# A transformer kernel in three-pass fp32: feed-forward input projections by seven half-size products, on one core

## What is computed

```python
def swiglu(h, w_in, w_out):                  # w_in 1024 x 5632, w_out 2816 x 1024
    gate, up = split(h @ w_in, 2)
    return (silu(gate) * up) @ w_out

# first block, latent tokens x (512 x 1024)
x = x + mod2 * rms_norm(gla_mixer(modulate(rms_norm(x), mod0, mod1)))
h = modulate(rms_norm(x), mod3, mod4)
x = x + mod5 * rms_norm(swiglu(h, ffn_w_in, ffn_w_out))         # ffn0
# second block
x = x + 0.5 * swiglu(rmsnorm(x) * g1, [ffn1_w1 ffn1_w3], ffn1_w2)   # ffn1
x = x + mixer(rmsnorm(x) * gm) @ w_out
x = x + 0.5 * swiglu(rmsnorm(x) * g2, [ffn2_w1 ffn2_w3], ffn2_w2)   # ffn2
return rmsnorm(x) * gf
```

## Time and profile before

| | before |
|---|---|
| three runs, median (us) | 1607.99, 1608.75, 1610.84; 1608.75 |
| span of the profiled execution (us) | 1607.1 |
| lies between the span and the median of the runs (us) | 1.65 |
| TensorE busy | 1596.4 us, 99% |
| VectorE, ScalarE, GpSimd busy | 849.0, 502.5, 119.9 us |
| the chain that ended last | TensorE 99% |
| DMA | 171.35 MB, 107 GB/s on average |

### The profile page before, as it was taken

One profiled execution on the slowest core, in us unless ns is written; L12 is line 12 of the kernel. 1 busy time (PEld: TensorE's weight loads), 2 busy tenths in 40 slices (PEclk: granted clock), 3 DMA queues, 4 the chain that ended last, 5 costly groups with the idle time before them and its releaser, 6 DMA issues.

```text
span 1607.1 us, 19314 instructions
## 1 busy us (share of the span) xinstructions
PE 1596.4 (99%) x7785; PEld 1343.6 (84%) x7785; DVE 849.0 (53%) x1050; ACT 502.5 (31%) x589; POOL 119.9 (7%) x106
## 2 busy tenths in 40 slices
...
GB/s 388 193 156 159 208 53 53 80 79 96 87 104 104 66 89 98 116 79 105 99 84 104 91 73 105 98 146 103 80 53 79 105 104 94 89 104 69 95 100 77
DMA packets 30647, 171.35 MB, mean 107 GB/s; under 512 B 3200, under 2 KB 5504, under 8 KB 17152
## 3 DMA queue, kind: packets, MB, share of 16 engines
...
HBM read 168.47 MB, written 2.10 MB: 106 GB/s over the span
## 4 chain that ended last, share of the span: by engine, by line
PE 99%; issue 0%; DVE 0%; POOL 0%; ACT 0%; POOLq 0%; DVEq 0%
PE bank L515 98%; PE bank L814 0%; PE bank L870 0%; POOL root L420 0%; PE bank L738 0%; PE bank L1143 0%; DVE y_ffn L2534 0%; ACT tmp L1500 0%; POOLq L123 0%; DVE qd L2111 0%; DVE kd L2111 0%; DVE tmp L2091 0%; DVE y_ffn L2532 0%; ACT mod_rows L1289 0%; DVEq L123 0%
## 5 line engine op out<-in xcount | busy, mean ns | idle before, releaser
L515 PE MATMUL bank<-a_hi,w_all 128*128 128x512 f32 x2490 | 764.7, 390 | 0.0
L515 PEld LDWEIGHTS bank<-a_hi,w_all 128*128 128x128 f32 x2490 | 466.5, 188 | 98.8 <-issue 2.5
L1712 DVE TENSOR_TENSOR w_all<-w_raw,w_all 128x2048 fp32r<-128x2048 f32 x140 | 323.3, 2309 | 360.5 <-ACT w_all L1265 360.3
L515 PE MATMUL bank<-a_lo,w_all 128*128 128x512 f32 x1245 | 477.1, 389 | 0.0
L1265 ACT ACTIVATE w_all<-w_raw 128x2048 fp32r<-128x2048 f32 x142 | 271.7, 1913 | 562.7 <-PE bank L515 562.7
L515 PE MATMUL bank<-g_hi,w_all 128*128 128x512 f32 (+1 forms) x1088 | 331.9, 386 | 0.0
L515 PEld LDWEIGHTS bank<-a_lo,w_all 128*128 128x128 f32 x1245 | 233.7, 188 | 48.8 <-issue 0.5
L515 PEld LDWEIGHTS bank<-g_hi,w_all 128*128 128x128 f32 x1088 | 203.9, 189 | 41.2
L515 PE MATMUL bank<-g_lo,w_all 128*128 128x512 f32 (+1 forms) x544 | 210.2, 386 | 0.0
L515 PEld LDWEIGHTS bank<-g_lo,w_all 128*128 128x128 f32 x544 | 102.5, 188 | 20.6
L515 PE MATMUL bank<-w_all,a_hi 128*128 128x512 f32 (+1 forms) x384 | 108.9, 359 | 0.0
...
## 6 DMA issues: line engine op xcount, KB each, us to landing
w_raw<-in_ffn_in SPq DMA_DIRECT2D x66, 1024.0 KB, 4.8
...
mod_raw<-in_mod POOLq DMA_DIRECT2D x16, 1024.0 KB, 5.6
...
w_raw<-in_gla_in SPq DMA_DIRECT2D x10, 1024.0 KB, 5.1
w_raw<-in_mix_in SPq DMA_DIRECT2D x10, 1024.0 KB, 4.7
mod_w<-in_mod SPq DMA_DIRECT2D x8, 1024.0 KB, 18.4
w_raw<-in_gla_out SPq DMA_DIRECT2D x4, 1024.0 KB, 4.7
```

The source lines that it names most:

```text
L515: return pe.matmul(out, lhs, rhs, start=first, stop=last, skip_group_check=True)
L1712: V.tensor_tensor(flat(w_lo[s]), flat(w_raw[s]), flat(w_hi[s]).bitcast(F32), ALU.subtract).then_inc(lo_done[s], 1)
```

## The change

Two of the eleven pairs of each feed-forward stay as they are. Pairs 2 to 10 are computed by Strassen's scheme in Winograd's form, over halves of k, halves of a unit's columns (c0, c1) and halves of the tokens, gate and up unit together: seven products, each of 4 k x 2 units x 3 passes = 24 matmuls of 128x256, 168 a pair. They use banks 0 to 3 (`PRODUCTS`).

- **Weights.** Seven forms of 128x1024: three are parts of the raw tiles, four are sums. GpSimd makes the first two sums (`form_sums`, one in place), VectorE the last two (`form_sum`). Each form is copied by ScalarE (`form_upper`) and subtracted by VectorE (`form_lower`) into a ring of four slots. SyncE loads the next pair's two raw tiles once `form_lower` 4 and 5 of this pair are done.
- **Activations.** Once in each feed-forward the scaled input `hs` (x by gain and roots, on VectorE in ffn1 and ffn2) gets four sums (`sum_x`) and is split into seven forms (`x_hi`, `x_lo`), while TensorE works on the plain pairs.
- **Results.** ScalarE copies four products out of PSUM (`snap`), VectorE makes the four quarters (`combine`), silu and the product work on 128x1024.
- **Output projection.** It runs in three parts of k: (0, 8) after pairs 2 to 4, (8, 16) after pairs 5 to 8, (16, 22) after pairs 9 and 10. Each part's sums are added by VectorE into `y_acc` or `xT`: 24 evictions a feed-forward, not 8. In ffn0 the norm's terms of all eight chunks come in the last part.
- `AHEAD` is gone; dummy matmuls (`keep_busy`) stand there. The loops over pairs are unrolled. In ffn0 ScalarE writes the modulated input twice, into `a_hi` and into `hs`.

The heads of the change:

```diff
-OUT_PARTS = ((0, 6), (6, 12), (12, 17), (17, 22))
...
+PLAIN = 2
+STRETCHES = ((2, 3, 4), (5, 6, 7, 8), (9, 10))
...
+OUT_PARTS = ((0, 8), (8, 16), (16, 22))
...
+PRODUCTS = ((0, True), (1, True), (0, False), (2, True), (0, False), (3, True), (2, False))
...
-AHEAD = (3, 4, 5)
```

SyncE's loads of the raw tiles inside a stretch, and GpSimd's two sums:

```diff
+if r:
+    sp.wait_ge(form_lo, FORMS * (n - 1) + 5 + h)
+else:
+    sp.wait_ge(hi_done[h], cnt.next(hi_done[h]))
+    sp.wait_ge(lo_done[h], cnt.next(lo_done[h]))
+w = slice(h * UNIT // 2, (h + 1) * UNIT // 2)
+sp.dma_start(raw_pair[h][:].rearrange("p u k o -> p u (k o)"),
+             w_in[2 * i:2 * i + 2, :, w].rearrange("u p w -> p u w")).then_inc(raw_loaded[h], 16)
...
+def form_sums(f):
+    for q, groups in enumerate(STRETCHES):
+        for i in groups:
+            n = PAIRS_PER_FFN * f + i - PLAIN
+            raw = 16 * (RAW_BEFORE[f] + PLAIN + i - PLAIN + 1 + 2 * q)
+            pool.wait_ge(raw_loaded[0], raw)
+            pool.wait_ge(raw_loaded[1], raw)
+            if i > PLAIN:
+                pool.wait_ge(form_lo, FORMS * n - 3)
+            nc.gpsimd.tensor_tensor(form_source(3), form_source(4), form_source(5), ALU.add).then_inc(form_summed, 1)
+            pool.wait_ge(form_summed, 4 * n + 1)
+            nc.gpsimd.tensor_tensor(form_source(4), form_source(0), form_source(4), ALU.add).then_inc(form_summed, 1)
```

TensorE's pair, and the dummies in place of the products ahead:

```diff
+def pair(q, r, i):
+    n = PAIRS_PER_FFN * f + i - PLAIN
+    first = i == PLAIN
+    for j, (b, fresh) in enumerate(PRODUCTS):
+        if first:
+            pe.wait_ge(xf_lo, FORMS * f + j + 1)
+        if j == 0:
+            if first:
+                gate_banks_free(i)
+            else:
+                pe.wait_ge(snapped, 4 * n)
+        elif j == 1 and not first:
+            pe.wait_ge(combined, 4 * n - 3)
+        elif j == 2:
+            pe.wait_ge(snapped, 4 * n + 1)
+        elif j == 3:
+            if first:
+                up_banks_free(i)
+            else:
+                pe.wait_ge(combined, 4 * n)
+        elif j == 4:
+            pe.wait_ge(snapped, 4 * n + 2)
+        elif j == 5 and not first:
+            pe.wait_ge(combined, 4 * n - 1)
+        elif j == 6:
+            pe.wait_ge(snapped, 4 * n + 3)
+        pe.wait_ge(form_lo, FORMS * n + j + 1)
+        slot = ring[(STRETCH_SLOT[q] + FORMS * r + j) % 4]
+        for k in range(KD // 2):
+            for u in range(2):
+                m = mm3(bank[b][:, HALVES[u]], (slot[:, 0, u, k], slot[:, 1, u, k]),
+                        (x_form[:, j, k, 0], x_form[:, j, k, 1]), fresh and k == 0 and u == 0, k == KD // 2 - 1)
+        m.then_inc(form_used, 1)
...
-    ahead_products(0, 0, AHEAD[0:2], True, False)
...
+keep_busy((4, 0)[n], (6, 12)[n])
```

ScalarE's pair:

```diff
+def pair(q, r, i):
+    n, last = PAIRS_PER_FFN * f + i - PLAIN, i == STRETCHES[q][-1]
+    form_upper(q, r, i, 3)
+    snap(n, snap_a, 0, 1, 4 * n - 3)
+    if r:
+        pair_silu(i - 1)
+    form_upper(q, r, i, 4)
+    form_upper(q, r, i, 5)
+    if r or q == 0:
+        product_hi(i - 1)
+    snap(n, snap_b, 0, 3, 4 * n)
+    form_upper(q, r, i, 6)
+    snap(n, snap_w, 2, 4, 4 * n - 2)
+    if not last:
+        form_upper(q, r + 1, i + 1, 0)
+    snap(n, snap_c, 0, 5, 4 * n - 1)
+    if not last:
+        form_upper(q, r + 1, i + 1, 1)
+        form_upper(q, r + 1, i + 1, 2)
```

VectorE: the input's sums, the weights' sums and low parts, the first quarters, the pair, the opening of a feed-forward, and the last part of its output (`p` counts pairs of chunks):

```diff
+def scale_x():
+    for m in range(KD):
+        V.scalar_tensor_tensor(hs[:, m], xT[:, m], gains(m), roots[:], ALU.mult, ALU.mult).then_inc(hs_done, 1)
+def sum_x():
+    dve.wait_ge(hs_done, X_STEPS * f + KD)
+    V.tensor_tensor(x_sum[:, 4, :, 1], x_quarter(1, 1), x_quarter(0, 1), ALU.subtract).then_inc(hs_done, 1)
...
+def form_sum(q, i, at):
+    n = PAIRS_PER_FFN * f + i - PLAIN
+    if at == 2:
+        dve.wait_ge(form_summed, 4 * n + 2)
+        dve.wait_ge(form_lo, FORMS * n + 1)
+        out, x, y = form_source(2), form_source(4), form_source(5)
+    else:
+        dve.wait_ge(form_summed, 4 * n + 3)
+        out, x, y = form_source(6), form_source(2), form_source(1)
+    V.tensor_tensor(out, x, y, ALU.add).then_inc(form_summed, 1)
+def form_lower(q, r, i, j):
+    n, slot = PAIRS_PER_FFN * f + i - PLAIN, ring[(STRETCH_SLOT[q] + FORMS * r + j) % 4]
+    dve.wait_ge(form_hi, FORMS * n + j + 1)
+    V.tensor_tensor(slot[:, 1], form_source(j), slot[:, 0].bitcast(F32), ALU.subtract).then_inc(form_lo, 1)
...
+def combine(n, quarter_at):
+    if quarter_at == 0:
+        dve.wait_ge(snapped, 4 * n + 1)
+        dve.wait_ge(form_used, FORMS * n + 2)
+        V.tensor_tensor(quarter(0, 0), by_unit(bank[1]), by_unit(snap_a), ALU.add).then_inc(combined, 1)
+    elif quarter_at == 1:
+        dve.wait_ge(snapped, 4 * n + 4)
+        V.scalar_tensor_tensor(quarter(1, 1), by_unit(snap_c), -1.0, by_unit(snap_w), ALU.mult, ALU.subtract).then_inc(combined, 1)
+    elif quarter_at == 2:
+        dve.wait_ge(form_used, FORMS * n + 6)
+        V.tensor_tensor(quarter(1, 0), by_unit(bank[3]), by_unit(snap_c), ALU.subtract).then_inc(combined, 1)
...
+def pair(q, r, i):
+    n, last = PAIRS_PER_FFN * f + i - PLAIN, i == STRETCHES[q][-1]
+    opening = i == PLAIN
+    if r:
+        combine(n - 1, 3)
+    elif opening:
+        ups(i - 1)
+        form_lower(q, r, i, 2)
+    form_lower(q, r, i, 3)
+    form_lower(q, r, i, 4)
+    if r or opening and scaled:
+        product(i - 1)
+    form_lower(q, r, i, 5)
+    if r or opening:
+        product_lo(i - 1)
+        dve.wait_ge(gated, GROUPS * f + i)
+    combine(n, 0)
+    form_lower(q, r, i, 6)
+    if not last:
+        form_lower(q, r + 1, i + 1, 0)
+        form_lower(q, r + 1, i + 1, 1)
+    else:
+        out_lower(q, 0)
+    combine(n, 1)
+    combine(n, 2)
+    if not last:
+        form_sum(q, i + 1, 2)
+        form_sum(q, i + 1, 3)
+        form_lower(q, r + 1, i + 1, 2)
...
+if f == 0:
+    sum_x()
+    split_lo(0)
+elif f == 1:
+    dve.wait_ge(roots_copied, cnt.next(roots_copied))
+    scale_x()
+    sum_x()
+    gates(0)
+    split_lo(0)
+else:
+    split_lo(1)
+    x_roots(5)
+    gates(0)
+    scale_x()
+ups(0)
+if f:
+    product(0)
+split_lo(1)
+if f == 2:
+    sum_x()
+x_lo(0)
+x_lo(1)
+product_lo(0)
 for j in range(2):
     V.memset(sq_sum[:, j * (T // 2):(j + 1) * (T // 2)], 0.0).then_inc(pair_out[j], 1)
     cnt.expect(pair_out[j])
...
+for j in range(2, FORMS):
+    x_lo(j)
+if scaled:
+    gates(1)
+first_forms(0, PLAIN)
...
+if f:
+    sum_pair((4 + 2 * j, 5 + 2 * j), CPU * p, True, j, f == 2)
+else:
+    for c in range(CPU):
+        m = CPU * p + c
+        dve.wait_ge(out_ready, cnt.next(out_ready))
+        V.tensor_tensor(y_acc[:, m], y_acc[:, m], bank[4 + 2 * j + c][:], ALU.add).then_inc(y_whole, 1)
+if p < 2:
+    out_lower(2, p + 2)
+elif p == 2 and f < 2:
+    split_lo(0)
+if f == 0:
+    for c in range(CPU):
+        m = CPU * p + c
+        done = pair_out[j] if c else chunk_done
+        cnt.expect(done)
+        y_terms_of(1, m, (done, cnt.now(done)), 2 * KD + m + 1)
```

More of the change, by code:

```diff
@@ L216, in build @@
         ret_sq_t = [place(f"ret_sq_t{s}", [P, T], F32, big + (64 + 2 * s) * KB) for s in range(2)]
-        tmp = [place(f"tmp{s}", [P, T]) for s in range(4)]
+        both = place("both", [P, 2, CPU, T])
+        tmp = [both[:, j // CPU, j % CPU] for j in range(4)]
         col4 = place("col4", [P, 16])
@@ L248, in build @@
         bank = [ctx.enter_context(nc.psum_tensor(f"bank{b}", [P, T], F32)) for b in range(8)]
-        ready = [sem(f"bank_ready{b}") for b in range(8)]
+        ready = [sem(f"bank_ready{b}") for b in range(6)]
         free = [sem(f"bank_free{b}") for b in range(8)]
@@ L1084, in half_roots @@
                 m.then_inc(roots_ready, 1)
[L1086 removed]
+            ffn(0)
             term_sums(1)
[L1088 to L1090 removed]
+            keep_busy(0, 20)
+            ffn(1)
             for n in range(6):
@@ L1541, in half_gains, with ffn, silu @@
                     nc.scalar.activation(y_ffn[:, m, h], xT[:, m, h], ACT.Copy, scale=col("final_g", m)).then_inc(y_gained, 1)
[L1543 to L1559 removed]
+            def ffn(f, next_gains=None):
+                scaled = f > 0
+                def silu(i):
@@ L2210, in x_roots, with sum_pair @@
                 dve.wait_ge(roots_copied, cnt.next(roots_copied))
-            def sum_pair(banks, chunks, half, to_x, j, squares):
-                dst = xT if to_x else y_ffn
-                at = [dst[:, chunks[c]] for c in range(CPU)]
-                if len(at[0].shape) == 3:
-                    at = [x.rearrange("p o t -> p (o t)") for x in at]
+            def sum_pair(banks, m0, half, j, squares):
                 for c in range(CPU):
```

673 lines of the change are left out of this document (376 added, 297 removed).

## The result

The changed kernel takes 1632.96 us (median of 4 runs, 1629.96 to 1639.28) against 1609.49 us before: ratio 1.0141, 95% interval 1.0118 to 1.0164. It is slower by 1.4%, and just above the range that was forecast. The profiled executions differ by 26.4 us (spans of 1633.5 and 1607.1); the medians differ by 23.5. What follows explains the 26.4.

What follows compares the result with a forecast made beforehand. TensorE, busy 1596.4 of 1607.1 us, was taken to bound the kernel. Saved 43.2 less lost 39.5 gave net -3.7, a span of 1603.4; with the median 1.65 above it, 1605 us, range 1583 to 1630.

Steps and rivals of the forecast that it cites:

- 27 pairs at 0.120 us a matmul: TensorE's changed pairs: 168 matmuls of 0.120 us, 20.16 us in place of 21.76, saving 43.2 us in all.
- loops inside stretches: Runs of changed pairs: the other engines' loop outlasts TensorE's pair; 11 us lost, bounds 0 and 56.
- ffn1's opening: TensorE waits for VectorE's split behind `scale_x` and `sum_x`, then for the first form; 7.0 us lost, bounds 4 and 10.
- ffn2's opening: VectorE reaches the first form at 1289, TensorE is ready at 1281; 8.3 us lost, bounds 3.5 and 11.
- ffn0's end: All norm terms fall into the last output part, so VectorE ends later after TensorE; 7.9 us lost, bounds 4 and 11.
- `AHEAD` gone: At ffn1's start, 18 matmuls (4.1 us) go back into the first pair; 1.3 us lost, bounds 0 and 4.1.
- last parts of ffn1, ffn2: Third weight part is split behind two evictions, 0.5 and 2.5 us after TensorE wants it; 3 us lost.
- lower clock: New waits of 6 to 8 us can bring TensorE's lower clock level twice more; 1 us lost, bounds 0 and 6.
- load 4.8 ... 21.45 us against TensorE's 20.16: The loop from one `form_lower` 5 to the next: raw tile load 4.8, then sums, forms, quarters; 21.45 us in all.
- no lock: Rival: GpSimd and VectorE don't exclude each other for these strided reads; loop 19.1 us, 1588 us in all; chance 0.20.
- the loop is longer and sets the pace: Rival: GpSimd sums of 2.6 us each make the loop 22.0, 1625 us in all (1650 with 3.3); chance 0.26.
- No saving at all: Rival: a new weight load every 0.12 us holds 128x256 matmuls back to 0.1295 us; 1648 us; chance 0.03.

Runs made afterwards that it cites:

- small_loads: The changed kernel, but from a stretch's second pair on each raw tile load brings only 64 of its 1024 elements a partition and unit; one run, 1602.8 us.
- sums_on_vector: The changed kernel, but from a stretch's second pair on VectorE forms all four weight sums; 1607.03 us against 1610.92 before, ratio 0.9974.

## Why the prediction was wrong, by its own steps

| step | said (us) | measured (us) |
|---|---|---|
| 27 pairs at 0.120 us a matmul | -43.2 | -43.2 |
| loops inside stretches | 11 | 32.0 |
| ffn1's opening | 7.0 | 9.2 (6.6 idle, 2.6 at the lower clock) |
| ffn2's opening | 8.3 | 9.3 (7.6 idle, 1.7 at the lower clock) |
| ffn0's end | 7.9 | 9.7 (join 7.6 longer, output projection 2.2) |
| `AHEAD` gone | 1.3 | 2.1 (ffn1's first pair 22.8, not 20.7) |
| last parts of ffn1, ffn2 | 3 | 5.8 (1.5 and 4.3) |
| lower clock | 1 | in the rows above: 2.6, 1.7, 1.7 in ffn2's last part, some 7 in the loops |
| ffn0's start (not named) | 0 | 1.3 |
| sum | -3.7 | 26.2 of 26.4 |

The mechanism was right, and the loop was mis-sized: it accounts for 21 of the 30 us between forecast and profile (some of it through the lower clock, below). The step that failed is "load 4.8 ... 21.45 us against TensorE's 20.16". Its chain from the landing on was priced at 16.65 us and took 16.7 (409.97 to 426.68). The load was priced by the earlier trace rows, a median over loads that mostly ran alone. Here the second tile is issued 2.3 us behind the first and lands after 5.1 to 6.5 us in ffn0 and ffn2, 6.9 to 8.1 in ffn1. Such a term enters every turn: past 20.16 each us of the loop is paid in each of the nine steady turns, and with ffn1's 24 us the lead of a stretch's second pair is gone too. The prediction said itself that the loop decides above 21.9; it took 22.5 in ffn0 and some 24 in ffn1. small_loads and sums_on_vector, each taking one part from the chain, gave back 30 and 26 us. The wait itself stood elsewhere than the prediction looked for it: at the third product, not at `form_lower` 5 or quarter 3.

The second miss was the clock. The waits were added up as idle time; four loop waits of 2.0 to 2.9 us, a wait of 2.3 in ffn2's last part and both openings were each followed by work at half clock, 1.3 to 2.6 us a time, where 1 us had been put in all. In the loops part of this only took the place of the next wait: the last two pairs of ffn1's second stretch took 24.8 and 24.1 us, the loop's own turns 24.0 and 24.3.

The openings, the joins and the last parts were right in mechanism and within 3 us each, though two readings were wrong. At ffn0's end the terms were said to have ended 2.0 us after TensorE's last product; after the last output product it was 3.3 us, so the same working gives 6.6, not 7.9, against 9.7. And of the 18 matmuls ahead only nine go back into the first pair (2.0 us): the 18 were nine products for each of two parts of the input. The lock between GpSimd and VectorE, against which the rival "no lock" stood, is there: `form_lower` 1 took 2.50 us beside a sum, the quarter 2.88. GpSimd's sums were priced at 2.1 and 2.6 and take 2.40 each without waiting, so that two errors cancel. The Trainium skill's page "GPSIMD Engine Reference" (Performance versus the Vector engine) measures 4.497 us for 2048 columns, by which 1024 would be 2.25 as an estimate; the trace has 2.40. Of the rivals, "the loop is longer and sets the pace" came true, but not by its price: the 2.6 us a sum were not the cause. The load was, which it named only as a point in its favour (two raw tiles at once, 5.6 us for the like); with 5.6 the loop would have been 22.25. "No saving at all" is refuted by the pitch of 0.120.
